# Gates of half the prompt tokens through a scatter-add table in HBM, their routing completed first

## What is computed

```python
def peer(xn, w_q, sub_keys, u_tab, v_tab):
    ...
    q = (xt @ w_q).reshape(n_tok, N_RHEADS, 2, D_HALF)           # 8 heads, two halves
    s = jnp.einsum('thpc,hpkc->thpk', q, sub_keys)               # 128 scores per half
    sv, si = lax.top_k(s, TOPK)                                  # 16 best of each half
    cand = sv[:, :, 0, :, None] + sv[:, :, 1, None, :]           # 256 candidates
    cand_idx = si[:, :, 0, :, None] * N_KEYS + si[:, :, 1, None, :]
    best, pos = lax.top_k(cand, TOPK)                            # 16 experts per head
    eidx = jnp.take_along_axis(cand_idx, pos, axis=-1)           # 128 experts per token
    g = jax.nn.softmax(best, axis=-1)
    ...
        act = jax.nn.gelu(jnp.einsum('ted,td->te', u, xblk))     # u = u_tab[experts]
        w = gblk * act
        return jnp.einsum('te,ted->td', w, v)                    # v = v_tab[experts]
```

## Time and profile before

| what | value |
|---|---|
| median of 3 runs | 2098.33 us (2097.99 to 2098.8) |
| profiled execution | 2098.75 us |
| its span in the trace | 2096.9 us |
| PE busy | 2055.7 us (98%) |
| DVE busy | 1635.7 us (78%) |
| ACT, POOL busy | 960.7 us (46%), 339.8 us (16%) |
| gate products on PE (L956) | 4608, 145.1 us |
| DMA | 358.34 MB, mean 171 GB/s |

### The profile page before, as it was taken

The page is one execution under the profiler, slowest core; times in us unless marked ns, Lnnn a source line. Parts: engine busy times, 40 slices in busy tenths (PEclk is TensorE's granted clock), DMA queues, the critical chain, the costliest instruction groups (busy, mean ns, idle before and its releaser), DMA issues.

```text
span 2096.9 us, 40394 instructions
## 1 busy us (share of the span) xinstructions
PE 2055.7 (98%) x16458; PEld 1889.3 (90%) x16458; DVE 1635.7 (78%) x3068; ACT 960.7 (46%) x1642; POOL 339.8 (16%) x245
## 2 busy tenths in 40 slices
PE   8999999999999999999999999999999999999998
PEld 7899999999889988887897999999998899888886
DVE  7887995555887688978799779965557777789776
ACT  5654553344433343445655545533334433444443
POOL 0014000000000064642110050000000000456420
PEclk9999999999999999999999999999999999999999
DMA  5354554444554457897322435544445544567873
GB/s 180 111 156 130 178 158 157 154 154 157 171 171 147 145 163 233 293 316 230 125 90 65 145 123 163 170 156 154 148 157 172 171 147 147 163 228 259 301 245 103
DMA packets 112935, 358.34 MB, mean 171 GB/s; under 512 B 17264, under 2 KB 27760, under 8 KB 112496
## 3 DMA queue, kind: packets, MB, share of 16 engines
q1 hardware_dynamic: 99888, 319.99, 47.2%
q0 software_dynamic: 12288, 33.60, 4.9%
q10 hardware_dynamic: 576, 2.18, 0.3%
HBM read 349.09 MB, written 6.63 MB: 170 GB/s over the span
## 4 chain that ended last, share of the span: by engine, by line
PE 84%; DVE 12%; ACT 2%; issue 2%; DMA 1%; SPq 0%; DVEq 0%; ACTq 0%
PE ps L878 15%; PE ps L879 14%; PE ps L880 14%; PE ps L909 11%; PE ps L910 10%; PE ps L911 10%; PE ps L956 6%; DVE w_lo L1470 2%; DVE work L1356 2%; DMA land<-stream_dram 1%; ACT w_hi L583 1%; PE ps L1037 1%; DVE hidden L1356 1%; DVE work L1364 0%; DVE hidden L1376 0%
## 5 line engine op out<-in xcount | busy, mean ns | idle before, releaser
L1470 DVE TENSOR_TENSOR w_lo<-land,w_hi 128x1024 fp32r<-128x1024 f32 x562 | 684.8, 1219 | 275.3 <-ACT w_hi L583 274.7
L583 ACT CAST w_hi<-land 128x1024 fp32r<-128x1024 f32 x592 | 621.2, 1049 | 441.1 <-PE ps L911 351.0
L878 PE MATMUL ps<-act_hi,w_hi 128*128 128x288 f32 x2688 | 809.2, 301 | 12.8 <-DVE act_lo L1196 5.9
L879 PE MATMUL ps<-act_hi,w_lo 128*128 128x288 f32 x2688 | 794.9, 296 | 0.0
L880 PE MATMUL ps<-act_lo,w_hi 128*128 128x288 f32 x2688 | 791.9, 295 | 0.0
L878 PEld LDWEIGHTS ps<-act_hi,w_hi 128*128 128x128 f32 x2688 | 505.4, 188 | 18.4 <-issue 10.9
L880 PEld LDWEIGHTS ps<-act_lo,w_hi 128*128 128x128 f32 x2688 | 507.7, 189 | 0.0
L879 PEld LDWEIGHTS ps<-act_hi,w_lo 128*128 128x128 f32 x2688 | 506.7, 188 | 1.0
L909 PE MATMUL ps<-w_hi,g_hi 128*128 128x512 f32 x1024 | 404.9, 395 | 3.6 <-DVE g_lo L1745 3.6
L910 PE MATMUL ps<-w_lo,g_hi 128*128 128x512 f32 x1024 | 399.1, 390 | 0.0
L911 PE MATMUL ps<-w_hi,g_lo 128*128 128x512 f32 x1024 | 398.8, 389 | 0.0
(11 more groups left out here) (214 smaller groups left out, 1353.8 us busy)
## 6 DMA issues: line engine op xcount, KB each, us to landing
land<-stream_dram SPq DMA_DIRECT2D x592, 512.0 KB
act_d<-smp_stage SPq DMA_DIRECT2D x64, 64.0 KB, 3.3
hidden<-stream_dram,smp_idx POOLq DMA_INDIRECT x128, 5.5
x<-x_dram SPq DMA_DIRECT2D x4, 288.0 KB, 6.8
y_t_dram<-hidden SPq DMA_DIRECT2D x8, 144.0 KB, 1.9
work<-keys_dram SPq DMA_DIRECT2D x1, 1024.0 KB, 7.5
smp_act<-act_d,smp_idx POOLq DMA_INDIRECT x64
work<-keys_dram ACTq DMA_DIRECT2D x1, 1024.0 KB, 9.0
```

What stands on the lines that cost most here:

```text
L583: nc.scalar.copy(w_hi[:, m, :], land[:, n % LANDS, :]).then_inc(w_hi_ready, 1)
L878: nc.tensor.matmul(out, w_hi[:, slot, wsl], hi, start=start, stop=False)
L879: nc.tensor.matmul(out, w_lo[:, slot, wsl], hi, start=False, stop=False)
L1470: V.tensor_tensor(w_lo[:, k, :], land[:, n % LANDS, :], w_hi[:, k, :].bitcast(F32), ALU.subtract).then_inc(lo_by_dve, 1)
```

## The change

The gates of prompt tokens 0 to 127 no longer go through one-hot chunks. A table `gates_d[L]` of 128 j x 128 tiles x 128 tokens f32 (8 MB for each layer) lies in HBM.

- **Zeroing.** ACT issues 16 DMAs of 1 MB that write zeros over both tables, in layer 0 behind slabs 3, 5, ... 33; POOL clears their source (2048 columns) at the start. DVE waits for all 16 before its first `first_level` of layer 0.
- **Adding.** When the picks of u = 0 are done, DVE computes addresses and copies the gates (`prepare_adds`); POOL issues 128 indirect DMAs a layer (`add_gates`), each of which adds 128 gates, one to a partition, into the table, with a wait for completion before every sixteenth. They stand ahead of `fetch_samples` in POOL's queue.
- **Loading.** SP loads the rows of two expert tiles (128 x 1 KB) into one of three buffers (`gate_land`), right behind the load of slab `APPLY_AT` + 4. The first waits for all adds.
- **Applying.** DVE multiplies them into `hidden` (`apply_pair`, 128 x 2 x 128), 64 times a layer, at slabs 134, 136, ... 164 and 180, 182, ... 274, ahead of `w_lo` of slab `APPLY_AT` + 3. ACT's `g_hi` waits for it.
- **Chunks.** Tokens 128 to 255 keep theirs: 32 a layer.
- **Routing.** DVE does all of u = 0 first; the order's constants move with it.

```diff
 GTOK = (16, 8, 16)
-GCH = [TP // t for t in GTOK]
+GTOK0 = (P, P, P)
+GCH = [(TP - t0) // t for t, t0 in zip(GTOK, GTOK0)]
...
+PAIRS = P // 2
+GATE_LANDS = 3
+FIRST_PAIRS = BLOCKS[0][1] // 2
+APPLY_AT = [(BLOCK_START[0] - 2 if k < FIRST_PAIRS else BLOCK_START[1] - 20 - 2 * FIRST_PAIRS) + 2 * k
+            for k in range(PAIRS)]
+ADDS = PICKS // HEADS
+ZERO_N, ZERO_W = 8, 2048
+ZERO_AT = [3 + 2 * z for z in range(DEPTH * ZERO_N)]
...
-TURN_AT = (75, 75)
-EXP_AT = (55, 68, 74)
-PICKS_AT = (76, 76)
+TURN_AT = (76, 76)
+EXP_AT = (52, 70, 75)
+PICKS_AT = (77, 77)
...
+                if r - 4 in APPLY_AT:
+                    k = APPLY_AT.index(r - 4)
+                    if k == 0:
+                        sp.wait_ge(gate_added, 16 * PICKS * (L + 1))
+                        sp.wait_ge(picks_ready, 3 * L + 3)
+                    if k >= GATE_LANDS:
+                        sp.wait_ge(pair_gated, PAIRS * L + k - GATE_LANDS + 1)
+                    two = slice(2 * k, 2 * k + 2)
+                    sp.dma_start(gate_land[:, k % GATE_LANDS, :],
+                                 gates_d[L][:, two, :].rearrange("j i t -> j (i t)")
+                                 ).then_inc(gate_landed[k % GATE_LANDS], 16)
...
+            def add_gates(L):
+
+                pool.wait_ge(adds_ready, L + 1)
+                pool.wait_ge(zeroed, 16 * DEPTH * ZERO_N)
+                cells = gates_d[L].rearrange("j i (t one) -> (j i t) one", one=1)
+                for k in range(PICKS):
+                    if k and k % ADDS == 0:
+                        pool.wait_ge(gate_added, 16 * (PICKS * L + k))
+                    nc.gpsimd.indirect_dma_start(
+                        out=cells, out_offset=bass.IndirectOffsetOnAxis(ap=add_idx[:, k:k + 1], axis=0),
+                        in_=add_val[:, k:k + 1], in_offset=None, compute_op=ALU.add).then_inc(gate_added, 16)
...
+            def zero(r):
+
+                if r in ZERO_AT:
+                    L, z = divmod(ZERO_AT.index(r), ZERO_N)
+                    act.wait_ge(zeros_ready, 1)
+                    rows = gates_d[L].rearrange("j i t -> j (i t)")
+                    act.dma_start(rows[:, z * ZERO_W:(z + 1) * ZERO_W], zeros).then_inc(zeroed, 16)
...
+                        act.wait_ge(pair_gated, PAIRS * L + e // 2 + 1)
                         nc.scalar.copy(g_hi[:, ring:ring + 2, :],
...
+            def apply_pair(L, k):
+
+                e, buf = 2 * k, k % GATE_LANDS
+                for half in range(2):
+                    dve.wait_ge(evacuated[half], L * USES + USE_U + (e + 2) // 2)
+                dve.wait_ge(gate_landed[buf],
+                            16 * (L * len(range(buf, PAIRS, GATE_LANDS)) + k // GATE_LANDS + 1))
+                two = hidden[:, e % HELD:e % HELD + 2, 0:P]
+                V.tensor_tensor(two, gate_land[:, buf, :].rearrange("p (i t) -> p i t", i=2), two,
+                                ALU.mult).then_inc(pair_gated, 1)
...
                 for b in range(4):
-                    for u in range(2):
-                        dve.wait_ge(scores_copied, SCORED * L + 2 * b + u + 1)
-                        first_level(L, u, 4 * b)
+                    first_levels(0, b)
                 next_lo()
+                second_level(L, 0, next_lo)
+                first_levels(1, 0)
+                soften(L, 0)
+                prepare_adds(L)
+                for b in range(1, 4):
+                    first_levels(1, b)
+                    if b % 2:
+                        next_lo()
                 dve.wait_ge(scores_copied, SCORED * (L + 1))
                 first_level(L, 2, 0)
                 did(V.tensor_copy(iota_rep, iota[:, :].unsqueeze(2).to_broadcast([P, KEYS, 2])))
-                second_level(L, 0, next_lo)
                 second_level(L, 1, next_lo)
-                soften(L, 0)
                 second_level(L, 2, some_lo)
...
                 for r in range(first, SLABS):
...
+                    while paired < PAIRS and APPLY_AT[paired] <= r:
+                        apply_pair(L, paired)
+                        paired += 1
```

More of the change, by code:

```diff
@@ L225, in build @@
         smp_act = sb("smp_act", [P, SMP])
+        tok_row = sb("tok_row", [P, 1])
+        gates_d = [nc.dram_tensor(f"gates_d{i}", (P, P, P), F32).ap() for i in range(DEPTH)]
         act_d = [nc.dram_tensor(f"act_d{i}", (P, P, TS), F32).ap() for i in range(DEPTH)]
@@ L304, in build @@
         iota_a = view(work_b, 2 * (E + 1744), TOPK, TOPK)
+        add_idx = rstd[:, 0:PICKS].bitcast(U32)
+        add_val = rstd[:, PICKS:2 * PICKS]
+        gate_land = view(work_f, E, GATE_LANDS, 2 * P)
+        zeros = view(flat, CAND_SLOT * TP, ZERO_W)
         def onehot_views(b, buf):
@@ L386, in build @@
         gated = sem("gated")
+        zeros_ready = sem("zeros_ready")
+        zeroed = sem("zeroed")
+        adds_ready = sem("adds_ready")
+        gate_added = sem("gate_added")
+        gate_landed = [sem(f"gate_landed_{k}") for k in range(GATE_LANDS)]
+        pair_gated = sem("pair_gated")
         g_hi_ready = sem("g_hi_ready")
@@ L489, in _ @@
                            allow_small_or_imprecise_dtypes=True).then_inc(consts_ready, 1)
+            nc.gpsimd.memset(zeros, 0.0).then_inc(zeros_ready, 1)
             pool.wait_ge(consts_ready, 4)
@@ L538, in _ @@
                 if n == TOTAL - 1:
+                    add_gates(1)
                     fetch_samples(1)
@@ L728, in layer @@
                     split(base + OUT0 + n + LEAD)
+                    if L == 0:
+                        zero(OUT0 + n)
                     if n:
@@ L747, in layer @@
                     split(base + Q0 + n + LEAD)
+                    if L == 0:
+                        zero(Q0 + n)
                     if n == 0:
@@ L1607, in apply, with prepare_adds @@
                 dve.wait_ge(expanded, g + 1)
-                tok = hidden[:, lo % HELD:lo % HELD + hi - lo, c * GTOK[b]:(c + 1) * GTOK[b]]
+                tok = hidden[:, lo % HELD:lo % HELD + hi - lo,
+                             GTOK0[b] + c * GTOK[b]:GTOK0[b] + (c + 1) * GTOK[b]]
                 V.tensor_tensor(tok, ps[:, GBANK + g % 2, 0:GTOK[b] * (hi - lo)].rearrange(
                     "p (t i) -> p i t", t=GTOK[b]), tok, ALU.mult).then_inc(gated, 1)
+            def prepare_adds(L):
+                did(V.tensor_scalar(add_val, picks_tok[:, 0, 0, :], float(P), tok_row[:, :], ALU.mult, ALU.add))
+                settle()
+                did(V.scalar_tensor_tensor(out=add_val, in0=picks_tok[:, 0, 1, :], scalar=float(P * P), in1=add_val,
+                                           op0=ALU.mult, op1=ALU.add))
+                settle()
+                did(V.tensor_copy(add_idx, add_val))
+                dve.wait_ge(picks_ready, 3 * L + 1)
+                settle()
+                V.tensor_copy(add_val, picks_tok[:, 0, 2, :]).then_inc(adds_ready, 1)
+            def apply_pair(L, k):
[7 more added lines that the diff above has]
+                                ALU.mult).then_inc(pair_gated, 1)
             def add_late(L, half):
@@ L1692, in peer @@
                     raw_q(n)
+                if L == 0:
+                    dve.wait_ge(zeroed, 16 * DEPTH * ZERO_N)
                 lo_next, skipped = [base + POOL_END], [0]
@@ L1732, in peer @@
                 settle()
-                made, applied, fetched = 0, 0, 0
+                made, applied, fetched, paired = 0, 0, 0, 0
                 first = lo_next[0] - base - LEAD
@@ L1769, in peer @@
                 add_late(L, 0)
-                assert made == applied == GATES
+                assert made == applied == GATES and paired == PAIRS
             split_lo(0)
@@ L1799, in _ @@
             did(V.tensor_reduce(smp_row[:, :], smp_num[:, 0, :], AX_X, ALU.add))
+            row_p = view(work_f, E, P)
+            did(V.tensor_tensor(row_p, ident[:, :], iota[:, :], ALU.mult))
+            settle()
+            did(V.tensor_reduce(tok_row[:, :], row_p, AX_X, ALU.add))
             did(V.tensor_copy(iota_a, iota[:, 0:TOPK].unsqueeze(2).to_broadcast([P, TOPK, TOPK])))
```

12 lines of the change are left out of this document (9 added, 3 removed).

## The result

The changed kernel takes 2167.84 us (median of 4 runs, 2166.51 to 2175.31) against 2098.16 us before: a ratio of 1.0339, 95% interval 1.0315 to 1.0363. It is slower by about 70 us, where 2114 us were forecast. The profiled execution took 2166.51 us, its span is 2164.7 us.

What follows compares the result with a forecast made beforehand. PE was taken to bound the kernel, so saved PE time and new PE waits count one to one: 2098.75 us with -68.2 + 44 + 33 + 3 + 3.5 = +15.3 gives 2114 us, range 2068 to 2146.

Steps and rivals of the forecast that it cites:

- The chunks, -68.2 us: PE's gate products: halving the chunks saves 34.1 us a layer, at 0.83 us per U chunk and 1.30 per V chunk.
- Routing, +44: First levels of u = 1 now run among U slabs, so PE waits for w_lo: 22 us a layer, 36 to 50 both.
- 17.7 us of waits to slab 66: PE's waits per layer for w_lo while DVE runs first levels among U slabs: 4.4 + 8.1 + 3.3 + 1.9.
- The turn: At the turn of the picks DVE has regained about 3 us of lead, so PE waits some 4 us more.
- the clock: PE's long waits in routing can drop its clock; a stretch costs up to 1.7 us, +2 in all.
- The new wait in the V stretch, +33: Last V stretch: apply_pair waits for gate loads in a loop of 6.5 us a pair; 0 if quiet, 58 at 7.0.
- 9 x 0.56 + 16 x 1.06 - 5.5 = 16.5: V-stretch loss per layer: 9 pairs with a chunk and 16 without, each over PE's time, less DVE's lead.
- DVE's lead in V slabs is 3 x 2.72 - 2.4 = 5.8, say 5.5, and is used up once: How far w_lo runs ahead of PE in V slabs, taken once as a cushion of 5.5 us a layer.
- The adds, "beside PE's work, if they end in time": POOL's 128 adds a layer cost PE nothing if done before SP needs the table near 515 us; expected done near 470.
- rival 3: POOL's adds end late and SP waits at slab 138, decisive from 2.0 us each; 2350 us at 3 us; chance 0.07.
- Smaller things, +6.5: Layer 1's keys and state +3, zeroing +1, PE's clock in routing +2, the start +0.5.
- Rival 1: Gate loads land quickly or the ring's lead covers the loop, no V-stretch loss: 2078 us, low end 2067; chance 0.33.

Runs made afterwards that it cites:

- e1: The changed kernel without the 256 adds and SP's wait for them, so gates of tokens 0 to 127 are missing: 2132.79 us.
- e5: e1 with both the old routing order and gate loads issued four slabs earlier: 2035.82 us, 0.9704 of the kernel before.
- e3: e1 with DVE's routing back in the old order, first levels of u = 0 and 1 in turn during the Q slabs: 2082.21 us.
- e2: e1 with each gate load issued four slabs earlier, behind slab A instead of A+4, same three buffers: 2082.60 us.
- e7: e1 with DVE's apply_pair moved from ahead of w_lo of slab A+3 to behind it: 2097.38 us.
- e4: The changed kernel with the 256 indirect DMAs writing their values instead of adding them, all waits kept: 2135.27 us.
- e6: The changed kernel, adds included, with the old routing order and gate loads four slabs earlier: 2123.27 us.
- c1: The changed kernel with old routing order, early gate loads, and the table only for tiles 32 to 127, first block keeping its chunks: 2053.59 us.

## Why the prediction was wrong

The direction was right, the size was not: +15 us were forecast, +68 came (profiled executions, 2098.75 and 2166.51), and 2167.84 lies outside the range of 2068 to 2146. Of the 52.5 us between, the adds make 29.8, the V stretch 22.2 and routing 9.2; the chunks and the smaller things take 8.7 of that back. Without the adds (e1, 2132.79 us) the time lies inside the range: the step that took it out is the price of an add.

- **The chunks, -68.2 us: right.** They gave 70.3 by the slab table, 1.3 a layer of it regained behind the turn, and 63 net of what is left of the rest (e5).
- **Routing, +44: right in mechanism, mis-sized.** 53.2 us came, and e3 took 50.6 of them away. The forecast's 17.7 us of waits to slab 66 were 19.2. The turn was taken for 4 us more of waiting than before, and 4.8 came; the term that was mis-sized is the clock, 2.6 us a layer behind the turn alone, for which the forecast had 2 us in all among its smaller things.
- **The new wait in the V stretch, +33: right in mechanism, mis-sized.** 55.2 came, e2 took 50.2 away. The term that was too small is "9 x 0.56 + 16 x 1.06 - 5.5 = 16.5"; 28.1 and 27.1 us were measured. Two of its numbers failed. The first is the pair, 6.80 and 6.57 us against 6.5: with these the same sum gives 24.0 and 18.2 us. Most of layer 0's surplus is the one landing beside layer 1's keys, for which the forecast had +3 apart. The second is "DVE's lead in V slabs is 3 x 2.72 - 2.4 = 5.8, say 5.5, and is used up once". This is the lead of `w_lo`. But behind the waiting `apply_pair` of slab A stands also `g_lo` of the visit at A+2, and PE wants that one slab sooner: in the trace of before it was ready 1.3 us (median) ahead of PE in slabs 226 to 274. With 1.3 in place of 5.5 the sums are 28.2 and 22.4: that covers layer 0 and leaves 4.7 us of layer 1 open. Single late pairs, whose time later ones didn't give back, may be that rest; no run shows it. Nor does a run change this lead alone: e7 leaves `g_lo` behind `apply_pair` and still gains 35 us, so the loop is the larger part, and the lead is read from the waits. The waits of the trace of before point there: of the few that PE had in V slabs, five were for `g_lo` and two for `w_lo`:

```profile
PE ps L909 <- DVE g_lo L1745: 3.6, 5, 2.1
...
PEld ps L909 <- DVE w_lo L1470: 3.4, 2, 2.5
```

- **The adds, "beside PE's work, if they end in time": wrong.** They were rival 3, with a chance of 0.07, and cost 29.8 us (e1: 35). The failed step is the price of one. I took the gather of the same shape, 1.17 us and 0.3 to the next, 215 us for 128. That price holds for an indirect DMA that only writes: e4's 128 took 213. An add takes 1.55 at best (e4 shows that the adding makes the difference), 1.75 in the mean, and with the waits 2.2. The point from which it decides was about right, 2.0 us: 128 x 0.2 = 26 us over, and SP, which came 10 us later than forecast, waited 14.6 and 20.4. What failed was to hold an unseen operation at the price of its nearest row with no upper end in the sum: a tenth of a microsecond an add was 13 us, and the margin was 45. The longest adds took 3.04 us, e4's longest write 3.03, so both kinds are stretched. The Trainium skill (SBUF — State Buffer, SBUF: two separate sides) says that GpSimd can't write its descriptors while DVE holds the port pair they share. The trace agrees: of the 256 adds the 190 that overlap one of DVE's TENSOR_TENSOR instructions took 1.82 us in the mean, the 66 others 1.54 to 1.75. This stretch has a part in the wait too. It makes 25 and 27 us of the two times 128 adds, and as an estimate from these rows, without it the adds would have ended before SP came. The gather's 1.17 us had such a stretch in it, but not the adding.
- **Smaller things, +6.5: the keys about right, the rest in other places.** Start and zeroing moved slab 60 by 1.3 us; DVE's first `first_level` waited 14.2 us for the zeros, in a stretch where it had waited for scores. In the old order, where eight first levels stand behind that wait, layer 0 loses 2 to 3 us from slab 40 to 60 (e3, e5, e6), and nothing in c1, which has 12 of the 16 zero DMAs and doesn't wait for them. Layer 1's keys and state pass inside the V stretch of layer 0, and are counted there: from slab 258 to 270 layer 0 lost 7.5 us and layer 1 5.0, in e1 10.4 and 5.6, in e7 5.7 and 0.9, against the +3.

Rival 1, with nothing lost in the V stretch, gave 2078 us (its low end of 2067 leaves out the +3.5; with it the sum is 2070). Its nearest run is e2, 2082.60, but without the adds. There ending the V stretch's loss does turn the sign, as was said; so does ending routing's (e3, 2082.21), which the forecast held between 36 and 50 us.

## What to carry to other kernels

Where an instruction on a busy in-order engine gets a wait, list all that stands behind it with the time at which each is wanted, and take the smallest slack as the cushion (here 1.3 us), not the one that is easiest to compute (5.5). A load that is waited for in a loop must be issued by something that doesn't stand behind that wait: four slabs earlier, with the same buffers, was worth 50 us. And price an operation that no trace shows by a range with an upper end, above all where its sum comes near a deadline.

## What the runs showed of the hardware

An indirect DMA of 128 values that adds into HBM holds POOL 1.55 us (median), one that writes 0.96 (e4), the shortest gather 0.94; beside DVE's TENSOR_TENSOR instructions adds and writes took up to 3.04 and 3.03 us. Gate loads of 128 rows of 1 KB, 64 KB apart in HBM, landed within 4.0 and 4.8 us of their issue beside the samples' fetch (903.03 to 907.03, 909.00 to 913.77), and one within 9.65 us beside 2 MB of other loads (953.61 to 963.26). And PE's granted clock fell to its lower level (0.50 in 327.30 to 337.60 us) in PE's waits of 5.3 to 9.8 us in routing and at the table of layer 0: the mean was 0.69 to 0.72 over the 17 to 22 us of those windows. It fell in the last V stretch too, where PE waited less at a time: 0.87 in the mean from 962 to 1002 us, with one wait of 5.88 us.
